# Finer waits in a convolution block, a shorter dispatch path in a router and weight halves split on another engine, in a two-layer kernel

## The reference, cut to what matters

```python
def first_block(x, ...):
    xn = rmsnorm(x, attn_norm_g)
    q_da, k_da, v_da, q_r, k_r, v_r, g_r = split(xn @ w_in)
    mix = concat([diff_attention(q_da, k_da, v_da, lam, ...), retention(q_r, k_r, v_r, g_r)])
    h = x + mix @ w_out
    return rmsnorm(h + hier_moe(rmsnorm(h, ffn_norm_g), ...), final_norm_g)

def hier_moe(xn, ...):           # group top-1, then expert top-2 within the group
    order = argsort(expert of each (token, choice))     # tokens of an expert, in blocks of 128
    for each block: y = (silu(xb @ w_gate[e]) * (xb @ w_up[e])) @ w_down[e]
    return sum over the two choices of weight * y

def conformer_conv(x, w_in, b_in, conv_w, conv_b, ln_g, ln_b, w_out, b_out):
    a, g = split(x @ w_in + b_in)
    h = a * sigmoid(g)
    h = depthwise causal convolution of h with 31 taps + conv_b
    return silu(layer_norm(h, ln_g, ln_b)) @ w_out + b_out

def second_block(x, ...):
    x = x + conformer_conv(rms_norm(x, mix_norm), ...)
    return x + square(relu(rms_norm(x, mlp_norm) @ w1)) @ w2
```

## Time and profile before

| what | value |
|---|---|
| median of 3 runs | 2100.85 us |
| the profiled execution's own time | 2099.99 us |
| its span | 2098.1 us |
| TensorE (PE) busy | 1946.9 us, 93% of the span |
| VectorE (DVE) busy | 1596.7 us, 76% |
| ScalarE (ACT) busy | 1061.7 us, 51% |
| GpSimd (POOL) busy | 547.8 us, 26% |

### The profile page before, as it was taken

The page is one execution under the profiler, slowest core; times in us unless marked ns, Lnnn a source line. Parts: engine busy times, 40 slices in busy tenths (PEclk is TensorE's granted clock), DMA queues, the critical chain, the costliest instruction groups (busy, mean ns, idle before and its releaser), DMA issues. The chain is left out here.

```text
span 2098.1 us, 29844 instructions
## 1 busy us (share of the span) xinstructions
PE 1946.9 (93%) x11025; PEld 1049.6 (50%) x11025; DVE 1596.7 (76%) x1688; ACT 1061.7 (51%) x1403; POOL 547.8 (26%) x350
## 2 busy tenths in 40 slices
PE   6999978799499999999994999959999999999999
PEld 5785436655245444444543555634544444444444
DVE  6866547744799999999987655485697898889876
ACT  6334327723488888888874554483332233332320
POOL 2222140000133333333320001021003665466530
PEclk9999999999699999999996999979999999999999
DMA  5111520061399999999996455437101112121112
GB/s 231 41 41 41 151 60 1 1 234 60 123 414 415 409 413 408 395 400 402 396 363 240 175 171 213 135 123 254 41 1 61 61 41 80 41 79 40 67 53 81
DMA packets 80914, 364.99 MB, mean 174 GB/s; under 512 B 14184, under 2 KB 27624, under 8 KB 48056
## 3 DMA queue, kind: packets, MB, share of 16 engines
q1 hardware_dynamic: 61880, 310.95, 38.0%
q0 software_dynamic: 18944, 52.80, 7.5%
HBM read 338.52 MB, written 37.75 MB: 179 GB/s over the span
## 5 line engine op out<-in xcount | busy, mean ns | idle before, releaser
L651 DVE SCALAR_TENSOR_TENSOR split<-stage,split 128x2048 f16<-128x2048 f32 x128 | 289.5, 2282 | 5.3 <-ACT split L647 3.4
L435 PE MATMUL ps<-split,xt 128*128 128x512 f16 (+1 forms) x776 | 289.6, 373 | 0.7 <-DVE xt L502 0.7
L436 PE MATMUL ps<-split,xt 128*128 128x512 f16 (+1 forms) x776 | 289.4, 373 | 0.0
L437 PE MATMUL ps<-split,xt 128*128 128x512 f16 (+1 forms) x776 | 289.3, 373 | 0.0
L647 ACT ACTIVATE split<-stage 128x2048 f16<-128x2048 f32 x128 | 240.5, 1904 | 94.4 <-PE ps L437 94.4
L1411 POOL TENSOR_TENSOR stage<-stage 128x1024 f32<-128x1024 f32 x48 | 134.0, 2792 | 267.3 <-DVE split L862 264.5
L435 PE MATMUL ps<-xt,split 128*128 128x512 f16 (+1 forms) x528 | 189.7, 359 | 6.7 <-issue 5.1
L436 PE MATMUL ps<-xt,split 128*128 128x512 f16 (+1 forms) x528 | 189.8, 359 | 0.0
L437 PE MATMUL ps<-xt,split 128*128 128x512 f16 (+1 forms) x528 | 189.4, 359 | 0.0
L651 DVE SCALAR_TENSOR_TENSOR arena<-arena 128x2048 f16<-128x2048 f32 x64 | 146.2, 2285 | 3.1 <-ACT arena L647 3.1
L857 ACT ACTIVATE split<-stage 128x1024 f16<-128x1024 f32 x56 | 57.3, 1048 | 143.3 <-PE pt L437 73.0
(11 more groups left out here) (543 smaller groups left out, 4772.5 us busy)
## 6 DMA issues: line engine op xcount, KB each, us to landing
stage<-in_w_gate SPq DMA_DIRECT2D x64, 1024.0 KB, 7.4
stage<-in_w_up SPq DMA_DIRECT2D x64, 1024.0 KB, 7.7
arena<-in_w_down SPq DMA_DIRECT2D x64, 1024.0 KB, 7.7
stage<-in_w_mlp SPq DMA_DIRECT2D x32, 1024.0 KB, 4.9
stage<-in_w_dense_a SPq DMA_DIRECT2D x16, 1024.0 KB, 7.3
arena<-in_conv_taps POOLq DMA_DIRECT2D x22, 640.0 KB, 5.2
stage<-in_w_dense_b SPq DMA_DIRECT2D x12, 1024.0 KB, 11.5
resid<-in_x SPq DMA_DIRECT2D x16, 512.0 KB, 6.9
```

The source lines that it names most:

```text
L435: nc.tensor.matmul(out_ap, lh, rh, start=start, stop=False)
L436: nc.tensor.matmul(out_ap, lh, rl, start=False, stop=False)
L437: return nc.tensor.matmul(out_ap, ll, rh, start=False, stop=stop)
L651: nc.vector.scalar_tensor_tensor(out=wlo(s), in0=wstage(s), scalar=WS, in1=whi(s), op0=ALU.mult, op1=ALU.subtract).then_inc(s_wo[s], 1)
```

## The change

- **Split halves.** The two GpSimd operations each for units 12 and 13 go. ScalarE makes the high half of 13 after the exponentials of attention block 1 instead of ahead of the attention. VectorE makes both low halves after the attention, behind the first transposed tile. Each tile of the output product takes its columns 512 to 1023 (units 14 and 15) first.
- **Router.** The token numbers of each expert's first block come straight from the rank: the 128 x 2048 comparison takes `rank` in place of `rpos`, the second matrix is the experts' one-hot times the token number, 16 matmuls of 32 columns fill `tok_of[:, 0:32]`, and `s_slots` goes to 1. The counts, places, starts and overflow numbers follow after that; the overflow blocks' one-hot matrices and numbers are made in the last two experts' turns (`over_slots`, `over_rows`, `over_tokens`).
- **First experts.** TensorE transposes the rows of expert 0 only before the first gate product, those of expert 1 after it; VectorE takes the low half of expert 0's rows before it splits the up weights.
- **Last convolution tile.** Each pair of groups of k = 7 gets a semaphore of its own, and TensorE waits pair by pair.
- **Rows of z.** SyncE reads phases 0 to 3 of every k, GpSimd phases 4 to 7, each of SyncE's phases with its own semaphore; TensorE waits for the phase it multiplies and for GpSimd's phases only behind the last k. GpSimd stores tile 1 before it reads tile 0 back. VectorE makes the low half of a tile before it centres a later one.

```diff
@@ def last_group(n):
-            return 7 if n < 4 else 15 if n < 12 else 30 + (n - 12) // 2
+            return 7 if n < 4 else 15 if n < 12 else 30 + (15 - n) // 2
@@ rows of z
-        def rows_back(eng, k, phases, landed):
-            for r in phases:
-                src = z_rows[k, CG * r:CG * r + CG, :].rearrange("c (q x) -> q c x", q=PH)
-                eng.dma_start(XT2[:, k, r, :], src).then_inc(landed, 16)
+        def row_back(eng, k, r, landed):
+            src = z_rows[k, CG * r:CG * r + CG, :].rearrange("c (q x) -> q c x", q=PH)
+            eng.dma_start(XT2[:, k, r, :], src).then_inc(landed, 16)
...
+        def landed_rows(k, r):
+            done, before = (((s_rp, 4), (s_rt, 4), (s_router_w, 32), (s_rd, 4)),
+                            ((s_lg, 1), (s_lx, 2), (s_rws, 1), (s_const, 16 * 11)))[k % 2][r]
+            return done, before + 16 * (k // 2 + 1)
+
+        def last_pair(i):
+            return ((s_rb[7], 16 * 3), (s_rx, 2 + 16 * 2), (s_zp[1], 16 * 2), (s_zp[0], 16 * 2))[i]
@@ def router(dve, ch):
+            for k in range(2):
+                V_.tensor_tensor(rB[:, k * TT:(k + 1) * TT, :], roh[k], bc(row[:, k, :], NE), ALU.mult)
+            V_.tensor_scalar(rthr[:, 0:7], iob[:, 1:8], float(P), None, ALU.mult)
             dve.wait_ge(s_rp, 1)
...
             rank = rrank.rearrange("p k t -> p (k t)")
+            V_.tensor_tensor(rA, io.unsqueeze(1).to_broadcast([P, 2 * TT, P]), bc(rank, P), ALU.is_equal)\
+                .then_inc(s_rt, 1)
...
+            dve.wait_ge(s_rp, 2)
+            rows = PS[:, 0, 0:NE]
...
+            V_.scalar_tensor_tensor(out=tok_of[:, 0:NE], in0=rows, scalar=2.0 * S, in1=rsec, op0=ALU.add, op1=ALU.add)\
+                .then_inc(s_slots, 1)
@@ def router(dve, ch):
-            V_.tensor_tensor(rA, io.unsqueeze(1).to_broadcast([P, 2 * TT, P]),
-                             bc(rpos.rearrange("p k t -> p (k t)"), P), ALU.is_equal)
-            ch.done(V_.tensor_tensor(rB, iob.unsqueeze(1).to_broadcast([P, 2 * TT, BLK_MAX + 1]),
-                                     bc(rblk.rearrange("p k t -> p (k t)"), BLK_MAX + 1), ALU.is_equal))
...
+        def over_slots():
+            V_ = nc.vector
+            nr = NOVER + 1
+            V_.tensor_tensor(rA_over, misc[:, M_IO:M_IO + P].unsqueeze(1).to_broadcast([P, 2 * TT, P]),
+                             bc(rpos.rearrange("p k t -> p (k t)"), P), ALU.is_equal)
+            V_.tensor_tensor(rB_over, iob_over.unsqueeze(1).to_broadcast([P, 2 * TT, nr]),
+                             bc(rblk.rearrange("p k t -> p (k t)"), nr), ALU.is_equal).then_inc(s_rd, 1)
@@ SyncE
+                if k < 7:
+                    rows_in(sp, k, range(PH), s_rb[k])
+                else:
+                    rows_in(sp, k, (0, 1), last_pair(0)[0])
+                    rows_in(sp, k, (2, 3), last_pair(1)[0])
...
-                rows_back(sp, k, range(4 if k == 0 else 5), s_rb[k])
+                for r in range(4):
+                    if k >= 2:
+                        sp.wait_ge(*landed_rows(k - 2, r))
+                    row_back(sp, k, r, landed_rows(k, r)[0])
@@ GpSimd
-            for i in range(2):
-                n = 12 + i
-                pool.wait_ge(s_wh[n % SLOTS], split_count(n))
-                nc.gpsimd.tensor_scalar(wstage(n % SLOTS), wstage(n % SLOTS), WS, None, ALU.mult).then_inc(s_pool, 1)
-                pool.wait_ge(s_pool, i + 2)
-                nc.gpsimd.tensor_tensor(wlo(n % SLOTS), wstage(n % SLOTS), whi(n % SLOTS), ALU.subtract)\
-                    .then_inc(s_wo[n % SLOTS], 1)
...
             rows_out(0)
+            rows_out(1)
             rows_last(0)
-            rows_out(1)
@@ ScalarE
-            for n in (12, 13):
-                split_hi(act, n)
+            split_hi(act, 12)
...
+                if b == 1:
+                    split_hi(act, 13)
@@ VectorE
+                if t == 1:
+                    for n in (12, 13):
+                        split_lo(dve, n)
...
             dve.wait_ge(s_gi, 2)
+            xe_lo(0, 0)
             for i in range(2):
                 expert_lo(dve, i, 0)
+            xe_lo(1, 1)
...
-                    for n in {0: (1, 2), KT - 2: (), KT - 1: ()}.get(k, (k + 2,)):
+                    for n in (1, 2) if k == 0 else ():
                         centred.append(centre(n))
                 if k:
                     dve.wait_ge(s_ch, k)
...
+                if 1 <= k < KT - 2:
+                    centred.append(centre(k + 2))
@@ TensorE
             pe.wait_ge(s_slots, 1)
-            for q in range(2):
-                x_transposes(q, q)
-            pe.wait_ge(s_slots, 2)
+            x_transposes(0, 0)
             pe.wait_ge(s_xel, 1)
             expert_product(pe, PS[:, 0, :], 2, 0, xeh[0], xel[0], s_g)
+            x_transposes(1, 1)
...
+                if last and q:
+                    pe.wait_ge(s_rt, 4)
+                    for n in range(2 * TT):
+                        i = nc.tensor.matmul(PT[:, 0, 0:NOVER + 1], rA_over[:, n, :], rB_over[:, n, :],
+                                             start=n == 0, stop=n == 2 * TT - 1)
+                    i.then_inc(s_rp, 1)
...
+                    if k == 7 and q % 2 == 0:
+                        pe.wait_ge(*last_pair(q // 2))
...
-                pe.wait_ge(s_rb[k], 16 * ((PH + 1 if k < 7 else 5) + (5 if k else 4)))
-                pe.wait_ge(s_cw[k % 2], 16 * pool_reads(k))
                 for t in range(TT // 2):
+                    pe.wait_ge(*landed_rows(k, t))
...
+            for k in (KT - 2, KT - 1):
+                pe.wait_ge(s_cw[k % 2], 16 * pool_reads(k))
```

More of the change, by code:

```diff
@@ L1083, in router @@
             ch.done(V_.tensor_tensor(rblk, rv, rix, ALU.add))
[L1084 to L1101 removed]
+            ch.done(V_.tensor_copy(rinc, PT[:, 3, NE:2 * NE]))
             ch.done(V_.tensor_tensor(rov[0:1], rinc[0:1, :].unsqueeze(1).to_broadcast([1, NOVER + 1, NE]),
@@ L1107, in router, with over_rows, over_tokens @@
             V_.tensor_copy(n_over, rinc[0:1, NE - 1:NE]).then_inc(s_slots, 1)
+        def over_slots():
[5 more added lines that the diff above has]
+                             bc(rblk.rearrange("p k t -> p (k t)"), nr), ALU.is_equal).then_inc(s_rd, 1)
+        def over_rows(dve):
+            V_ = nc.vector
+            dve.wait_ge(s_rd, 3)
+            for k in range(2):
+                part = rB_over[:, k * TT:(k + 1) * TT, :]
+                i = V_.tensor_tensor(part, part, bc(row[:, k, :], NOVER + 1), ALU.mult)
+            i.then_inc(s_rt, 1)
+        def over_tokens(dve):
+            V_ = nc.vector
+            dve.wait_ge(s_rp, 4)
+            rows = PT[:, 0, 0:NOVER + 1]
+            V_.tensor_scalar(rsec_over, rows, -float(S), -float(S), ALU.is_ge, ALU.mult).then_inc(s_rd, 1)
+            dve.wait_ge(s_rd, 4)
+            V_.scalar_tensor_tensor(out=tok_of[:, NE:BLK_MAX + 1], in0=rows, scalar=2.0 * S, in1=rsec_over,
+                                    op0=ALU.add, op1=ALU.add)
+            V_.tensor_scalar(dest_of[:, NE:BLK_MAX + 1], rows, 2.0 * S, None, ALU.add).then_inc(s_slots, 1)
         @block.sync
@@ L1399, in rows_last @@
                     pool.wait_ge(s_cw[k % 2], 16 * pool_reads(k - 2))
-                rows_back(pool, k, range(4 if k == 0 else 5, PH), s_cw[k % 2])
+                for r in range(4, PH):
+                    row_back(pool, k, r, s_cw[k % 2])
             rows_out(0)
+            rows_out(1)
             rows_last(0)
-            rows_out(1)
             for k in range(1, KT):
@@ L1660, in body @@
                 act.wait_ge(s_g, e + 1)
-                if not (first and q == 0):
+                if first and q == 0:
+                    act.wait_ge(s_slots, 2)
+                else:
                     act.wait_ge(s_h, e)
@@ L2107, in _ @@
                     dve.wait_ge(s_x[t], 32)
-                    for c in range(2):
-                        g = 16 + 2 * t + c
+                    for j, c in enumerate((1, 0)):
+                        g = 16 + 2 * t + j
                         dve.wait_ge(s_full[g % 4], g // 4 + 1)
@@ L2123, in _ @@
             router(dve, ch)
-            dve.wait_ge(s_gi, 2)
-            for i in range(2):
-                expert_lo(dve, i, 0)
             def xe_lo(e, q):
@@ L2132, in xe_lo @@
                 nc.vector.tensor_tensor(xel[q], tpair(0), xeh[q], ALU.subtract).then_inc(s_xel, 1)
-            for q in range(2):
-                xe_lo(q, q)
+            dve.wait_ge(s_gi, 2)
+            xe_lo(0, 0)
+            for i in range(2):
+                expert_lo(dve, i, 0)
+            xe_lo(1, 1)
             expert_lo(dve, 4, 0)
@@ L2161, in body @@
                         expert_lo(dve, s, e + 2)
+                if last and not q:
+                    over_slots()
                 if not (last and q):
                     expert_lo(dve, 4, e + 1)
+                if last and not q:
+                    over_rows(dve)
             pairs(body, dve)
@@ L2783, in body @@
```

(8 more changed lines are left out.)

95 lines of the change are left out of this document (43 added, 52 removed).

## The result

The changed kernel took 2079.24 us (median of 4 runs, 2078.22 to 2080.79) against 2100.74 for the kernel before: a ratio of 0.991 with a 95% interval of 0.9897 to 0.9922. The medians of the changed kernel agree within 0.1 us; that of the kernel before moved by 4, and on two more occasions it was 2095.58 and 2095.77. So there are two questions: how much of the 21.5 us is the change, and how much is where TensorE's clock happened to fall in the execution that the prediction was made from.

What follows compares the result with a forecast made beforehand. TensorE, 93% busy, was taken as the bound, waiting on chains elsewhere in four places on one path. Gains of 5.5, 3.4, 4.1 and 2.6 us sum to 15.6, giving 2085.3 us on the median's scale; range 2081 to 2092.

Steps and rivals of the forecast that it cites:

- C: Split halves of units 12 and 13, around the attention: net gain 5.5 us, bounds 4 and 7.
- D: Router and first experts: earlier dispatch and first gate product, gain 3.4 us, bounds 0.8 and 4.95.
- A: Last convolution tile: TensorE starts on the first pair of rows, gain 4.1 us, bounds 3.2 and 5.7.
- B: Rows of z: first z product starts 2.6 to 3.0 us earlier; gain 2.6 taken, bounds 1.5 and 3.5.
- 6.4 more, where only GpSimd's splitting differs: Attention's first head against the third, first to fourth `subtract_map`: 16.68 against 10.32 us, the difference expected back.
- 0.8 net: High half of 13 moved behind block 1's exponentials: gain bounded at 1.6 us, 0.8 left as delay of block 2.
- some 1.2, I take 1.3: After the attention: TensorE stalls 1.3 us because VectorE's two low halves stand before tile 2's rows.
- 10 to 13 assumed: First gate product: 10 to 13 of TensorE's 24 products at half clock, coming cold from idle.
- its rival: Gathers ahead of the expert loop: held at 3.70 us beside VectorE, D gives 0.8, time 2087.9; chance 0.05.
- The stream's rival: Expert loop: set by the weight stream, so D's 3.4 us are returned, time 2088.7; chance 0.06.
- A row lands some 2.4 behind its issue: Last convolution tile: landing time read from GpSimd's last issue, giving TensorE's start 3.2 us earlier.
- It should not fall in 1.9: Last convolution tile: idle shrinks from 5.12 to 1.9 us, so TensorE's clock stays up; 0.9 us gained in the tile.
- The slower side: Rows of z: waiting phase by phase holds TensorE's clock at 1.2 GHz, + 41 us, time 2127; chance 0.04.

Runs made afterwards that it cites:

- both_first: Changed kernel, but TensorE transposes the rows of experts 0 and 1 both ahead of the first gate product; 2078.46 us against 2095.77, ratio 0.9915.
- plus: Changed kernel, with VectorE's low half of 13 behind tile 3's rows and expert 1's transposes between the first gate product's halves; 2077.12 us, ratio 0.9901.
- plus_rows: `plus`, with GpSimd's reads of the last tile ahead of a load of taps; 2077.62 us against 2095.77 for the kernel before, ratio 0.9908.
- the second occasion: Changed kernel, unchanged, run again beside the kernel before; 2079.15 us against 2096.95, ratio 0.9916.
- c_hi_ahead: Kernel before with the split-halves change alone, but both high halves kept ahead of the attention; 2093.4 us against 2095.58, ratio 0.9982.
- before_fill: Kernel before with 16 small matmuls added ahead of the last expert's wait for its hidden rows' low half; 2097.3 us against 2095.58, ratio 1.0006.

## Why the prediction was right, and where not

The means over the traces, stage by stage, against the terms of the sum:

| term | forecast | measured | from |
|---|---|---|---|
| C, up to the router | 5.5 | 5.4 | counting matmuls: mean 535.7 in seven traces without C (533.8 to 537.3), 530.4 in four with it |
| D, from there to the last expert's wait | 3.4 | 4.4 to 4.7 | with C 560.6 in two traces without D, 556.2 in two with it; without C 559.4 in six, 554.7 in one |
| C, in the same stretch | 0 | -1.2 to -1.5 | the same four numbers, compared the other way |
| A, idle and last tile | 4.1 | 2.9 | 15.9 in eight, 13.0 in five |
| B, statistics to z | 2.6 | 3.3 | 20.0 in seven, 16.8 in five |
| sum | 15.6 | 14.8 | the changed kernel against the kernel before: 5.4, 3.2, 2.9 and 3.3 |

(The second and third row leave out `both_first`, `plus` and `plus_rows`, whose edits lie in that stage.) That the sum comes within 1 us is partly luck: D and B were sized too small, A too large, and C loses time behind the router, for which there was no term. Between the last expert's wait and the last tile no part has an edit but the 16 matmuls of the overflow blocks, and the forecast has no term. Yet this stage takes 266.9 and 267.1 us in the changed kernel's two traces and 268.0 to 272.2, mean 269.8, in the twelve others: another 2.8. With it the stages make 17.6 of the 17.8 by which the medians differ on the second occasion. It is where three of the four places of the table above lie. Whether the changed kernel keeps its clock there by something in its code, or by chance in both traces, is not shown; `both_first` and `plus` speak for chance. The trace that the prediction was made from takes 272.2 there, and 1.6 more in the second head, which is most of what the first measurement's 21.5 has beyond 17.8.

**Part C.** The mechanism is right: `c_hi_ahead` shows it with nothing else changed in the first head. The step that failed is "6.4 more, where only GpSimd's splitting differs". The clock differed too, 0.78 to 0.89 in the first head against 1.00 in the third. What GpSimd cost is 3.3 to 4.1 us: from the first to the fourth `subtract_map` all seven traces without C take 16.7, and all seven without GpSimd's arithmetic 12.6 to 13.3. This was made up by the high half of 13, for which the sum had 0.8 net and which gave 1.9, and by the second head: three of the seven traces without C have the fall of the clock there, the one of the prediction among them, and none with C, which is some 0.7 of the 5.4. The stall of "some 1.2, I take 1.3" measured 1.3 (96.46 against a mean of 95.2 in seven traces without C, 94.8 to 95.5, between the same two points), and `plus` shows that it could be had for nothing. What the sum had no term for is the loss of 1.2 to 1.5 behind the router. With C the first gate product starts 0.4 later behind the counting matmuls, and 8 or 9 of its matmuls are slow in place of 3 or 4 (with D on both sides, 14 in place of 8). But `before_fill`, without C, has 8 as well; whether C or chance holds the clock down longer there stays open.

**Part D.** Each step came where it was put: matmuls 6.1 earlier (5.9), gather 6.0 (5.9), gate product 8.3 (8.2), `hbuf` 3.0 (3.4 to 3.8) in that one pair of traces; with C or without on both sides the stage gains 4.4 to 4.7. Half pace lasted for the first 13 products, the upper end of the 10 to 13 assumed. One reading of the rows was wrong and did no harm: the counting at 541.50 starts right behind the complete rank (541.46), not 0.8 before it.

The gather at 1.09 refutes its rival, and two readings behind that rival were wrong. VectorE was not idle beside the gather of 1.10 at 551.98, it ran small instructions until 552.59; beside an idle VectorE the second gather took 1.00. And the store at 3.70 is an exception. Of the 65 indirect DMAs in the trace of before 60 overlap a 128 x 2048 SCALAR_TENSOR_TENSOR of VectorE by more than 0.1 us, 31 of them by more than 0.9, and 58 of the 60 took 1.0 to 1.4; only two, at 580.81 and 587.32, took 2.46 and 3.70. What sets those two apart is not shown. The Trainium skill's "SBUF — State Buffer", the box on the "DVE blocks DMA" trap, has a DMA issued from GpSimd wait while VectorE runs an operation that holds the port both share; no gather ahead of the loop shows such a wait, neither beside the small instructions nor beside the TENSOR_TENSOR of 1.2 us (1.02 at 545.09 and at 556.49 in the changed kernel). Whether the two long ones are such waits no run here tests.

The stream's rival is refuted as well: from first to last expert the shift stayed 10.2 us. I priced expert 1's transposes behind the gate product as part of the sum, and rightly, but did not ask for the other order. By the traces, this edit is better split than undone.

**Part A.** The step that failed is "A row lands some 2.4 behind its issue". That was read off GpSimd's last read, counted from the start of its issue, and applied to SyncE's first pair from the end of an issue. From the end of its second issue that pair lands 3.8 later, when 640 KB of taps go out 0.4 us after its first; without them in front it is 2.3 (`plus_rows`). So the idle time gave 2.4 and not 3.2, and the tile 0.5 and not 0.9. "It should not fall in 1.9" held only by half: the idle time was 3.2 to 3.3, and the clock fell within the tile, 0.9 to 1.4 us after its start in the five traces.

**Part B.** "2.6 to 3.0; I take 2.6" measured 3.3: 0.8 for VectorE's order and 2.5 for the rest. SyncE's first row is used 2.96 behind its issue, just below the assumed 3.0 to 3.4. The slower side (clock held low by waiting in pieces) did not arise: there is no pause at any k, and the stretch behind takes 648.1 as before.

**The range** of 2081 to 2092 lies just above the result. It was made from the bounds of the terms, with the trace's execution taken to stand for the kernel, and had no term for that execution itself being slow. A second trace of before would have shown a spread of 5.4 us in the span.

## What to carry to other kernels

A stretch of the same kernel is a yardstick for another only at the same granted clock. The clock alone doesn't mend it (10.32 divided by 0.89 is 11.6, and 12.60 was measured), and neither does adding up the stretched instructions (7.9 us longer, of which 3.3 to 4.1 were on the path); a kernel with only that work taken out does. Where gains of 3 us are at stake and a kernel's runs spread over 9, measure the distance between two fixed points on the bounding engine in several traces; it told A's 2.9 us from nothing where twelve runs hardly did. Compare only traces that differ in nothing else: the mean of all eight traces without D against that of the three with it gives 4.0 us for D, since C is in two of the eight and in two of the three; like against like gives 4.4 to 4.7. And see whether the traced execution is like the others (`plus_rows`). And when work is moved behind a long product, see what waits for it: with the product split and the short work in between (`plus`), `hbuf` came 30.4 us behind the counting matmuls, against 31.5 and 34.2 for the two orders.

## What the runs showed of the hardware

- GpSimd's arithmetic on 128 x 2048 float32 stretched VectorE's SCALAR_TENSOR_TENSOR instructions beside it by a factor of 3.4 to 5.8 (1.15 to 3.90, 0.35 to 2.02), and three such stretches on the path cost 3.3 to 4.1 us.
- An indirect DMA issued from GpSimd took 1.09 and 1.01 beside VectorE instructions of 0.2 to 0.4 us, and 1.00 beside none. Beside those of 128 x 2048, 2.28 us long, 58 of 60 took 1.0 to 1.4 and two took 2.46 and 3.70.
- Behind idle times of 1.8 to 2.2 us, and in the second head behind none longer than 1.01, TensorE's clock falls to half in some executions of the same code and not in others, sometimes only a microsecond into the work behind. Sixteen small matmuls in the gap did not prevent it. What decides it stays open.
